# A block with RWKV, attention and a product-key expert layer: 160 instead of 128 tokens fetch their rows, and 88 blocks of a table are turned beside the first projection

## What is computed

```python
proj = x @ w_in[i]
...
expert_idx = jnp.take_along_axis(cand_i, best_pos, axis=-1)
gate = jax.nn.softmax(best_s, axis=-1)
...
u = jnp.take(expert_u, ic, axis=0)
act = jax.nn.gelu(jnp.einsum('cd,cjd->cj', xc, u), approximate=False) * gc
return jnp.einsum('cj,cjd->cd', act, jnp.take(expert_v, ic, axis=0))
```

## Time and profile before

| | |
|---|---|
| time, median of 3 runs | 5098.11 us (5096.62 to 5098.44) |
| profiled execution: its time, its span | 5100.68 us, 5099.0 us |
| granted TensorE clock, mean of the span | 0.938 |
| busy: PE, weight loads, DVE, ACT, POOL | 4453.5, 3965.4, 3163.2, 1543.0, 1613.2 us |
| instructions | 60536 |
| DMA | 909.28 MB, mean 178 GB/s |
| projection | from the start to about 992 us |
| gate matrix | about 2602 to 2812 us |
| experts | 2812.9 to 5034 us |

### The profile page before, as it was taken

The page is one execution under the profiler, slowest core; times in us unless marked ns, Lnnn a source line. Parts: engine busy times, 40 slices in busy tenths (PEclk is TensorE's granted clock), DMA queues, the critical chain, the costliest instruction groups (busy, mean ns, idle before and its releaser), DMA issues. The chain is left out here.

```text
span 5099.0 us, 60536 instructions
## 1 busy us (share of the span) xinstructions
PE 4453.5 (87%) x23108; PEld 3965.4 (78%) x23108; DVE 3163.2 (62%) x4666; ACT 1543.0 (30%) x2477; POOL 1613.2 (32%) x976
## 2 busy tenths in 40 slices
PE   8999999865766498889965599999999999999995
PEld 6888888623435487677754599999999999999995
DVE  2222222266993443469458588888888888888885
ACT  2111111134441232222322233333333333333332
POOL 0000000000452000033520255555555555555552
PEclk9999999976778799999999799999999999999997
DMA  4333333236105443234315998989888898999883
GB/s 157 115 119 123 123 123 123 79 117 149 36 19 168 157 139 143 74 121 137 120 48 159 287 260 263 262 259 261 260 260 261 260 262 262 262 261 261 261 254 128
DMA packets 556411, 909.28 MB, mean 178 GB/s; under 512 B 44680, under 2 KB 398832, under 8 KB 518928
## 3 DMA queue, kind: packets, MB, share of 16 engines
q1 hardware_dynamic: 518672, 635.62, 43.1%
q0 software_dynamic: 36864, 268.45, 16.2%
q10 hardware_dynamic: 640, 2.10, 0.1%
HBM read 809.51 MB, written 96.56 MB: 178 GB/s over the span
## 5 line engine op out<-in xcount | busy, mean ns | idle before, releaser
L102 PE MATMUL h_ps<-h_xs,h_ut 128*128 128x384 f32 x6144 | 1152.8, 335 | 69.0 <-DMA h_xs<-xs_d 62.1
L102 PE MATMUL h_ps<-h_a,h_v 128*128 128x384 f32 x6144 | 1154.1, 335 | 34.5 <-DVE h_a L96 34.5
L102 PEld LDWEIGHTS h_ps<-h_xs,h_ut 128*128 128x128 f32 x6144 | 1078.2, 189 | 71.3 <-DMA h_xs<-xs_d 62.3
L102 PEld LDWEIGHTS h_ps<-h_a,h_v 128*128 128x128 f32 x6144 | 1070.9, 188 | 44.7 <-DVE h_a L96 44.7
L96 POOL TENSOR_TENSOR h_v<-h_v_raw,h_v 128x512 fp32r<-128x512 f32 x512 | 766.9, 1498 | 872.0 <-ACT h_v L95 869.9
L102 PE MATMUL a_ps<-a_xt,a_w 128*128 128x512 f32 x4224 | 960.0, 390 | 7.7 <-DVE a_w L96 7.7
L102 PEld LDWEIGHTS a_ps<-a_xt,a_w 128*128 128x128 f32 x4224 | 794.6, 188 | 172.8 <-issue 7.9
L96 DVE TENSOR_TENSOR h_ut<-h_u_turn,h_ut 128x512 fp32r<-128x512 f32 x512 | 352.3, 688 | 389.9 <-ACT h_ut L95 389.6
L95 ACT ACTIVATE h_v<-h_v_raw 128x512 fp32r<-128x512 f32 x512 | 322.5, 630 | 588.4 <-PE h_ps L102 588.4
L95 ACT ACTIVATE h_ut<-h_u_turn 128x512 fp32r<-128x512 f32 x512 | 323.7, 632 | 569.9 <-PE h_ps L102 469.3
L96 DVE TENSOR_TENSOR a_w<-a_raw,a_w 128x2048 fp32r<-128x2048 f32 x88 | 201.2, 2288 | 452.9 <-issue 230.6
(11 more groups left out here) (306 smaller groups left out, 5341.4 us busy)
## 6 DMA issues: line engine op xcount, KB each, us to landing
h_u_raw<-in_peer_u SPq DMA_DIRECT2D x512, 256.0 KB
h_v_raw<-in_peer_v SPq DMA_DIRECT2D x256, 512.0 KB
a_raw<-in_w_in SPq DMA_DIRECT2D x44, 2048.0 KB
sums_d<-g_grid SPq DMA_DIRECT2D x3, 8192.0 KB
h_gt<-sums_d SPq DMA_DIRECT2D x128, 192.0 KB
proj_t<-a_ob SPq DMA_DIRECT2D x44, 512.0 KB, 2.8
o_raw<-in_w_o SPq DMA_DIRECT2D x16, 1024.0 KB, 5.0
f_raw<-in_peer_w_q SPq DMA_DIRECT2D x8, 2048.0 KB
```

The source lines that it names most:

```text
L102: mm = pe.matmul(out, lhs[a], rhs[b], start=(first and n == 0), stop=(last and n == 2))
```

## The change

- 32 more tokens (of tile 1) fetch rows, 160 in all; 352 are dense. The 128 choices of the 32 tokens are folded four to a job: 32 jobs of 32 tokens x 4 choices, besides 128 jobs of 128 tokens. JOBS = 160, 320 fetches of 1 MB in place of 256. `SLOTS` sets at which of 16 quarters DVE uses a row (ten of them); POOL issues the fetch of row r + 4 before that quarter's lower half of v. `route` writes index and gate of the 32 tokens and moves them by eight small DMAs; `finish` adds the four partial sums with a matmul by `fold`.
- Beside the projection, SP loads 88 of the 128 blocks of u (1 MB each) into what was `xin`, DVE turns them (four transposes a block) and SP stores them to `turned_d`. In the expert stage a turned block comes in 4 KB pieces and ACT and DVE split it as loaded; 40 blocks are turned there as before. `block_of` spreads them: the fourth step of each group is always such a "raw" one, the third from s = 98 on.
- Three of the 16 chunks of the result (`KEPT`) accumulate in PSUM banks of their own through all 32 groups and are copied out at the end. The other 13 share four banks (before: six for all). The hidden activations have one bank (bank 0, before two) and one SBUF tile.
- The weights of u and v have three buffers (`WR`) in place of four and are made three quarters ahead; u's raw data comes in halves with three buffers, v's in whole steps with two, in 2 KB pieces.
- The gate matrix makes 88 units in place of 96. Rows of `xs_d` and the gate matrix have 352 numbers.
- The lower halves of v are on POOL in both kernels.

```diff
+            def load_u(q, r):
+                for z in range(4):
+                    src = uv[q, z] if isinstance(q, int) else uv[bass.ds(q, 1), z].rearrange("b i g j -> (b i) g j")
+                    sp.dma_start(u_raw[r][32 * z:32 * z + 32, :, :], src).then_inc(u_in[r], 16)
+
+            def store_u(q, r):
+                sp.wait_ge(u_turned, q * Q + Q)
+                dst = turned_d[q] if isinstance(q, int) else \
+                    turned_d[bass.ds(q, 1)].rearrange("q p c e -> (q p) c e")
+                sp.dma_start(dst, u_turn[r]).then_inc(u_stored[r], 16)
...
             with sp.Fori(0, NQ // 4 - 1) as i:
-                for u in range(2):
-                    sp.wait_ge(lo_done, i * 4 + (2 * u + 2))
-                    sp.dma_start(raw[u][:, :, :], wv[bass.ds(i * 2 + (2 + u), 1)].rearrange("g p k c -> (g p) k c"))\
-                      .then_inc(raw_in[u], 16)
-                for u in range(2):
-                    store(i * 2 + u, u, ov[bass.ds(i * 2 + u, 1)].rearrange("g p b t -> (g p) b t"))
-            for u in range(2):
-                store(NQ // 2 - 2 + u, u, ov[NQ // 2 - 2 + u])
+                for s in range(4):
+                    if s % 2 == 0:
+                        sp.wait_ge(lo_done, i * 4 + (s + 2))
+                        sp.dma_start(raw[s // 2][:, :, :],
+                                     wv[bass.ds(i * 2 + (2 + s // 2), 1)].rearrange("g p k c -> (g p) k c"))\
+                          .then_inc(raw_in[s // 2], 16)
+                    store_u(i * 4 + s, s % 2)
+                    load_u(i * 4 + (s + 2), s % 2)
+                    if s >= 2:
+                        store(i * 2 + (s - 2), s - 2, ov[bass.ds(i * 2 + (s - 2), 1)].rearrange("g p b t -> (g p) b t"))
...
+                if odd:
+                    eng.wait_ge(u_in[s % 2], i * 128 + 64 * (s // 2 + 1))
+                    eng.wait_ge(u_stored[s % 2], i * 32 + 16 * (s // 2 + 1))
+                    for c in range(Q):
+                        turn(eng, u_turn[s % 2][:, Q * c:Q * c + Q, :], u_raw[s % 2], c).then_inc(u_turned, 1)
...
+FOLD = 4
+FEW = P // FOLD
+FETCH = P + FEW
+DENSE = T - FETCH
+JOBS = SEL + SEL // FOLD
+KEPT = 3
...
+            sp.wait_ge(sm.sem, sm.at(0, "gate_few"))
+            for f in range(FOLD):
+                rows, cols = slice(f * FEW, (f + 1) * FEW), slice(f * SEL // FOLD, (f + 1) * SEL // FOLD)
+                sp.dma_start(fetch_idx[1][rows, :], few_idx[:, cols]).then_inc(few_moved, 16)
+                sp.dma_start(fetch_gates[1][rows, :], few_gates[:, cols]).then_inc(few_moved, 16)
...
+                sp.wait_ge(grid_kept, NQ * (n + 1) - SKIP)
+                first = FETCH - P if n == 0 else 0
+                t = P * (n + 1) - FETCH
+                sp.dma_start(gv[:, :, t + first:t + P], grid[n % 2][:, :, first:P]).then_inc(grid_stored[n % 2], 16)
...
-    CH = KT
-    HB, YB = 2, 6
-    AR, RR, VR = 7, 3, 3
+    GROUPS = STEPS // GRP
+    CH, ADDED = KT, KT - KEPT
+    YB = 7 - KEPT
+    AR, RR, UR, VR, WR = 7, 4, 3, 2, 3
+    SLOTS = (1, 2, 3, 5, 6, 7, 9, 10, 11, 13)
...
-        ut = [[sb(f"ut{p}{r}", [P, Q, P], F32R) for r in range(Q)] for p in range(2)]
-        v_raw = [sb(f"v_raw{r}", [P, GRP, 2 * P]) for r in range(VR)]
-        v = [[sb(f"v{p}{r}", [P, GRP, P], F32R) for r in range(Q)] for p in range(2)]
+        ut = [[sb(f"ut{p}{r}", [P, Q, P], F32R) for r in range(WR)] for p in range(2)]
+        v_raw = [sb(f"v_raw{r}", [P, GRP, Q * P]) for r in range(VR)]
+        v = [[sb(f"v{p}{r}", [P, GRP, P], F32R) for r in range(WR)] for p in range(2)]
...
-        gt = [sb(f"gt{r}", [P, DENSE]) for r in range(2)]
-        hid = [sb(f"hid{r}", [P, DENSE]) for r in range(2)]
+        hid, gt = yt_last[0], yt_last[1:]
...
+        def block_of(s):
+
+            return s % GRP * GROUPS + s // GRP
+
+        def is_raw(s):
+
+            return block_of(s) >= TURNED
...
+        def uses_at(n):
+
+            return n // 16 * 10 + SLOTS.index(n % 16) if n % 16 in SLOTS and n < Q * STEPS else None
...
+        def bank_of(y):
+
+
+            g, c = divmod(y, CH)
+            n = g * ADDED + min(c, ADDED)
+            return (1 + n % YB if c < ADDED else 1 + YB + c - ADDED), n
...
+            def load_u(h):
+                s = h // 2
+                if h >= UR:
+                    sp.wait_ge(u_lo, 2 * (h - UR) + 2)
+                b = block_of(s)
+                half = slice(h % 2 * (Q * P // 2), (h % 2 + 1) * (Q * P // 2))
+                if is_raw(s):
+                    for z in range(4):
+                        sp.dma_start(u_raw[h % UR][32 * z:32 * z + 32, :].rearrange("p (g f) -> p g f", g=4),
+                                     uv[b, z][:, :, half]).then_inc(u_in[h % UR], 16)
+                else:
+                    sp.dma_start(u_raw[h % UR][:, :].rearrange("p (c e) -> p c e", e=P),
+                                 turned_d[b][:, h % 2 * KT // 2:(h % 2 + 1) * KT // 2, :]).then_inc(u_in[h % UR], 16)
 
             def load_gate(s):
...
-                        pe.wait_ge(u_lo, Q * s + q + 1)
-                        if q == 0 and s >= HB:
-                            pe.wait_ge(gelu_done, s - HB + 1)
+                        n = Q * s + q
+                        pe.wait_ge(u_lo, n + 1)
+                        if q == 0 and s >= 1:
+                            pe.wait_ge(gelu_done, s)
                         for k in range(Q):
                             d = Q * q + k
-                            mm = product(pe, ps[:, s % HB, 0:DENSE], [ut[h][q][:, k, :] for h in range(2)],
+                            mm = product(pe, ps[:, 0, 0:DENSE], [ut[h][n % WR][:, k, :] for h in range(2)],
...
+                        bank, n = bank_of(y)
                         pe.wait_ge(v_lo, y + 1)
-                        if y >= YB:
-                            pe.wait_ge(y_added, y - YB + 1)
+                        if c < ADDED and n >= YB:
+                            pe.wait_ge(y_added, n - YB + 1)
...
-                split(nc.scalar, nc.vector, "hi", v_raw[hv % VR][:, :, (q % 2) * P:(q % 2 + 1) * P], v[0][q][:, :, :],
-                      None, v_hi)
...
+                act.wait_ge(v_in[s % VR], 16 * (s // VR + 1))
+                if y >= WR:
+                    act.wait_ge(y_made, y - WR + 1)
+                split(nc.scalar, nc.vector, "hi", v_raw[s % VR][:, :, q * P:(q + 1) * P], v[0][y % WR][:, :, :], None,
...
             for s in range(last):
                 for q in range(Q):
+                    n = Q * s + q
                     if q == 0 and 1 <= s <= STEPS:
                         hidden(s - 1)
                         hidden_half(s - 1)
-                    if s + 1 < STEPS:
-                        u_half(s + 1, q)
-                    if GRP <= s + 1 < last:
-                        v_half(s + 1 - GRP, q)
-                    if q == 2 and s < SEL:
-                        choice(s)
+                    r = uses_at(n - 1)
+                    if r is not None and use(r)[0]:
+                        choice(use(r)[1])
+                    t, z = divmod(n + WR, Q)
+                    if t < STEPS:
+                        u_half(t, z)
+                    t, z = divmod(n - Q * GRP + WR, Q)
+                    if 0 <= t < STEPS:
+                        v_half(t, z)
...
+                c = y % CH
+                if c >= ADDED:
+                    return
                 dve.wait_ge(y_made, y + 1)
...
+                    if n >= Q * GRP + 1:
+                        add(n - Q * GRP - 1)
+                    t, z = divmod(n + WR, Q)
+                    if t < STEPS:
+                        u_rest(t, z)
+                    r = uses_at(n)
+                    if r is not None:
+                        use_row(r)
...
+            dve.wait_ge(y_made, Q * STEPS)
+            dve.wait_ge(a_lo, STEPS)
+            for i in range(KEPT):
+                dve.tensor_copy(yt_last[i][:, :], ps[:, 1 + YB + i, 0:DENSE]).then_inc(y_kept, 1)
...
+            pool.wait_ge(xs_in, 32)
+            for r in range(RR):
...
+            for n in range(Q * last):
+                r = uses_at(n)
+                if r is not None:
+                    fetch(r + RR)
+                t, z = divmod(n - Q * GRP + WR, Q)
+                if 0 <= t < STEPS:
+                    v_rest(t, z)
...
+                    if n == 1:
+                        pe.matmul(ps[0:FEW, j % 8, :], fold[:, :], y_few[:, T * g:T * (g + 1)], start=True, stop=True)
...
+                        part = yt[:, d, here] if d < KT - KEPT else yt_last[d - KT + KEPT][:, here]
+                        if n == 1:
+                            for p in range(FEW, P, FEW):
+                                t = max(p - FEW, 0)
+                                tr = pe.matmul(ps[p:p + FEW, j % 8, i * P:(i + 1) * P], part[:, t:t + FEW], ident[:, :],
+                                               start=True, stop=True)
...
+    turned_d = dram("turned_d", [TURNED, P, KT, P])
```

(29 more changed lines are left out.)

291 lines of the change are left out of this document (156 added, 135 removed).

## The result

| | before | after |
|---|---|---|
| time, median | 5097.98 us (5096.62 to 5098.44, 4 runs) | 5305.76 us (5302.02 to 5307.76, 4 runs) |
| profiled execution: its time, its span | 5100.68, 5099.0 us | 5306.91, 5304.9 us |
| granted clock, mean of the span | 0.938 | 0.921 |
| busy: PE, DVE, ACT, POOL | 4453.5, 3163.2, 1543.0, 1613.2 us | 4385.4, 3580.2, 1524.3, 1338.3 us |

After over before is 1.0407, 95% interval 1.0389 to 1.0425: slower, where 5074 us (5030 to 5170) was forecast. DVE has 417 us more of busy time, though 352 transposes went from the expert stage to the projection without changing their number.

The account below looks back on a forecast made before the run. PE was taken to bound projection and expert stage. The terms summed to -23.9 us on the profiled execution's 5100.7 us, giving 5076.8; that execution being 2.6 us above the median, the forecast was 5074 us, range 5030 to 5170.

Parts of the forecast that it names:

- Columns: Expert stage, PE: matmuls of 352 columns take 0.160 us instead of 0.1733; 1.28 us less a step, -158.7 us.
- rival (c): Expert stage: fewer columns bring nothing, as weight loads keep a matmul at 0.1733 us; 5235 us, chance 0.05.
- Gelu wait: Expert stage: with one bank for hidden activations, PE's next h block waits for ACT's gelu; 1.37 us a step, +169.9 us.
- Group wait: Expert stage: PE's 1.04 us wait at each group's start for the last hidden tile disappears; 30 waits, -31 us.
- So DVE is hidden: Expert stage: DVE's fullest step adds up to 16.5 of 16.73 us, so DVE does not delay PE.
- Late only if DVE lags some 6 us: Expert stage: POOL's lower half of v, waiting for a row's use, is late only if DVE lags some 6 us.
- Rival (d): Expert stage: each step grows by another wait, DVE or DMA late by 1 us; 5198 us, chance 0.07.
- First four steps: Start of expert stage, DVE-bound: three steps need no turning now, but rows are fetched only after `xs`; -2 us.
- Projection: New DMA work for u beside PE's blocks, 10.95 us against 10.88 a block: +12 us; transposes and store at its end: +6.
- Rival (a): Projection: the DMA queue becomes the bound at 12.1 us a block, +107 instead of +12; 5169 us, chance 0.18.
- Start: Start of the experts: PE's wait for its first loads shrinks to some 17 to 18 us; -12.5 us.
- Routing, gate matrix and its store: Before the experts: eight small routing DMAs +3.5 us, eight fewer gate matrix units -14.5, the gate matrix's last store +4.

## Why the prediction was wrong, by its own steps

- **Columns**: 0.160 us a matmul, measured 0.161; -149 us for -158.7. Right, and rival (c) is out.
- **Gelu wait**: 1.37 us a step; measured 1.53 (1.47 late, 0.06 in the block behind) in three steps of four, and +152 us for +148 with the bank alone. Right within its bounds. But its upper bound, "1.6 us if ACT is sometimes late with the choice of a row", does not hold for the fourth step, which is 5.9 us late for just that reason.
- **Group wait**: gone, as said.
- **"So DVE is hidden" is the step that failed.** It added the fullest step up to 16.5 of 16.73 us, from durations of the kernel before, and took them as properties of the operations. They were properties of the operations beside what POOL did then. The sign was in its own rows: the gate product took 1.65 us beside POOL's lower half of 1.98 us; apart they take 0.52 (at 352 columns) and 1.29. The prediction used the 1.65 and did not ask what made it, and so not where that cost goes when POOL's order changes. The Trainium skill, "SBUF — State Buffer", section "SBUF: two separate sides", has the rule: a VectorE operation with two SBUF inputs and a GpSimd operation that reads SBUF exclude each other, and the one that comes second stands still. The traces agree that one of the two stands still: the `h_ut` of 2.15 us ends at 4056.94, 0.56 us behind the end of POOL's operation (4056.38), and alone it takes 0.69. On which one that is they differ from the words: the record of this `h_ut` begins 0.30 us before POOL's.
- **"Late only if DVE lags some 6 us"** asked whether the wait of POOL's fetch for DVE's row use makes v late. It does not. It lines POOL up with DVE, and that does the harm.
- **The lag's way to PE** was priced nowhere: the choice ahead of `u_half`, `v_half` and the gelu on ACT, with one bank to wait for. Of a wait of 6.5 us on ACT, 4.2 us more than the ordinary 1.4 reach PE, and the slow blocks behind it add 2.8 us in the group shown, 2.1 on average. Rival (d), "another wait, DVE or DMA late by 1 us in each", had the form and half of the size, and 0.07.
- **First four steps**: -2 forecast, +11.4 measured. With one bank the gelu waits stand in the start too (4.82, 1.90, 6.38 and 2.94 us), beside one of 10.33 us for `h_ut`.
- **Projection**: +12 forecast inside the stage, nothing measured; +5.1 at its end for +6. Rival (a), at 0.18, is out. **Start**: -13.1 for -12.5. **Routing, gate matrix and its store** together: -10.2 for -7. The last store of the grid took 31.2 us in both kernels (from its issue to the experts' first, 2781.73 to 2812.91 and 2775.46 to 2806.64), so neither the +4 taken for it nor the +8 estimated by the Trainium skill's rule is there. **Finish**: +3.5 for +2.

## To carry to other kernels

A duration read from a trace includes who stood beside it; where an order or a wait of GpSimd changes, list VectorE's two-input operations and ask which of them GpSimd's next one will meet, since a wait of one on the other lines them up in every round. An engine's average share (DVE 81%) says little about a step whose work is booked to 99%, and work handed to GpSimd can cost VectorE more than doing it. Where one buffer stands behind an activation, that activation belongs ahead of everything on its engine that waits for a third.
